# A split-precision decoder trunk on one core: another order of the seven block products in its MLP, with norm and sample work moved

## The chip, the core and the metric

The kernel runs on one core of one Trainium2 chip. The core has TensorE (matmuls into PSUM), VectorE, ScalarE, GpSimd and SyncE (SP, which here only issues DMAs), each with its own instruction queue; they meet by semaphores. The metric is the device time of one execution in microseconds (us), lower is better.

## What is computed

One step of a decoder trunk for 1024 prompt tokens and 32 sample tokens, all in float32. Mixing heads and an output projection come first; the change lies in the MLP and the last norm behind them:

```python
x = x + mix.astype(x.dtype) @ w_out
u = rmsnorm(x, g_ffn) @ w_up                  # 1024 -> 4096
x = x + jnp.square(jax.nn.relu(u)) @ w_down   # 4096 -> 1024
y_prompt = rmsnorm(hp, g_final)               # x of the prompt
y_sample = rmsnorm(hs, g_final)               # x of the sample tokens
```

## The kernel before

A float32 operand is cut in two: a high part in the format that TensorE multiplies fast (a copy with rounding, on ScalarE) and a low part, which is the operand less its high part. A product is then three matmuls, low by high, high by low, high by high. So each operand needs a high instruction on ScalarE and a low instruction on VectorE or GpSimd before TensorE can start.

The MLP (`phase_g_*`) goes through the 4096 hidden columns in 8 blocks (`NBLK`) of 4 chunks of 128 columns (`NF`). A block has two parts.

*Hidden pieces.* 12 pieces (`NU`), three token groups of 352 for each chunk (`hidden_piece`, `product`, L340 to L342). VectorE takes each from PSUM with a ReLU (L2669) into R_u, ScalarE squares it there (L2531, `squared`). Chunks of w_up arrive in R_stage, ScalarE makes their high part (L2075, `up_high`) and GpSimd the low part (L2079, `up_low`). In the last chunk of a block the groups go 2, 0, 1.

*The product with w_down.* The 32 sample tokens have a product of their own in bank 7 (`sample_product`, L350). The prompt's product is a 2 by 2 block product in seven multiplications in place of eight (Winograd's form of Strassen's scheme), the steps P1 to P7. Their left operands are quarters of R_u (q11 to q22: token half, column half) or sums of them (s2 = q22 - q21 on VectorE, L2675; three others on GpSimd), the right ones quarters of w_down in R_raw (w11 to w22) or sums of them on GpSimd (T_1 to T_4; t2 lies in R_stage). The order is P1 P2 P6 P7 P5 P3 P4. A step is four token tiles p of six matmuls (`step`, L2510 to L2512), 24 in all. Some steps open their PSUM banks, others add to what an earlier step left there; after each step VectorE adds the bank to x1 in SBUF (`added`, L2659; P7's twice, to two places). For each step ScalarE makes the high parts (left L2546, right L2554). VectorE makes the left low parts (L2649) and P6's right low part (L2686), GpSimd the other right low parts (L2600). High parts have two buffers by turns, so a step's high parts wait for the step two before it.

What sets the order is the code itself: each engine's list is written out, and `operand_high`, `right_split`, `dve_split`, `pool_sums`, `d_psum` and `d_taken` are the semaphores between them. The sample product stands behind the last piece and ahead of P1, GpSimd's weight sums wait for it (they write over R_raw), and so the sums start with P1.

*Start and end.* Four small DMAs bring the final norm's gain for the sample tokens (`g_sample`); SP issues them behind two chunks of w_up and four row blocks of w_down. VectorE waits for them ahead of the MLP's first ReLU:

```python
            dve.wait_ge(x1_in, 16 * 17)
            for b in range(NBLK):
```

At the end `final` norms the nine token tiles in the order sample, 0 to 7, within and behind P4: a sum of squares on ScalarE (L2589), mean (L2639), root on ScalarE (L2591), reciprocal (L2642), multiply (L2644), and SP stores the tile. The sample's mean needs one small matmul (L2524) that sums over token rows, between P3 and P4.

Of the kernel before, what the change touches and what calls it, by code (L numbers as in the profile page):

```python
# [151 lines left out]
def program(nc, i_, o_):  # L152

    ctx = ExitStack()
    with ctx:
# [257 lines left out]
        def phase_a_act(act):  # L413
# [33 lines left out]
            act.wait_ge(small_dve, 1)  # L447
# [54 lines left out]
        def phase_a_pe(pe):  # L502
# [15 lines left out]
            pe.wait_ge(bias_ready, 1)  # L518
# [183 lines left out]
        def phase_b_act(act):  # L702
# [110 lines left out]
        def phase_b_sync(sp):  # L813
            for s in range(NSLOTS):
# [15 lines left out]
                if s == 13:  # L830
                    sp.wait_ge(small_dve, 3)
# [1513 lines left out]
        def quarter(ap, j, i, n):  # L2345
# [18 lines left out]
        POOL_LOWS = (P1, P2, P7, P5, P3, P4)  # L2364
        S_3, T_1, T_2, T_3, T_4, S_1, S_4 = range(7)
        HIGH_ORDER = [(P1, "right"), (P2, "right"), (P1, "left"), (P2, "left"), (P6, "left"), (P6, "right")] + [
            (k, side) for k in (P7, P5, P3, P4) for side in ("right", "left")]
        DVE_ORDER = [(P1, "left"), (P2, "left"), (P6, "left"), (P6, "right"), (P7, "left"), (P5, "left"), (P3, "left"),
                     (P4, "left")]
# [4 lines left out]
        dve_split, s2_ready, pool_sums = sem("dve_split"), sem("s2_ready"), sem("pool_sums")  # L2374
# [3 lines left out]
        LAST_TILES = [NCH, 0, 1, 2, 3, 4, 5, 6, 7]  # L2378
# [46 lines left out]
        def phase_g_sync(sp):  # L2425
# [13 lines left out]
            for b in range(NBLK - 1):  # L2439
# [13 lines left out]
            for done, i in enumerate(LAST_TILES):  # L2453
# [139 lines left out]
        def phase_g_gps(pool):  # L2593
# [8 lines left out]
            for b in range(NBLK):  # L2602
# [25 lines left out]
                if not last:  # L2628
                    up_low(NF * b + 6)
# [148 lines left out]
```

## Time and profile before

| what | us |
|---|---|
| median of 3 runs (lowest, highest) | 1548.35 (1547.43, 1549.69) |
| the profiled execution, its span | 1547.07, 1545.3 |
| TensorE matmuls busy | 1455.8 (94%) |
| VectorE busy | 889.2 (58%) |
| GpSimd busy | 562.8 (36%) |
| ScalarE busy | 508.8 (33%) |

The profile is of one execution, with times counted from its first instruction. In rows and listings PE is TensorE, DVE VectorE, ACT ScalarE, POOL GpSimd and SPq SP's DMA queue. A timeline row gives start, duration, engine, line, output and inputs, and in brackets how long the engine stood idle ahead of it and what released it. Consecutive instructions of an engine overlap a little, so starts tell the pace better than durations do. Matmuls overlap more: a step matmul shows 0.39 us, but the next starts 0.23 later. The MLP runs from about 800 to 1528 us.

### The profile page before, as it was taken

Reading aid. Unit: us, or ns where it says so; the run is one execution under the profiler, and the core shown is the slowest. Engines: PE = TensorE matmul, PEld = TensorE weight load, DVE = VectorE, ACT = ScalarE, POOL = GpSimd, SP = SyncE. Lnnn points to the kernel's source line nnn. Section 1 sums busy time; section 2 is a strip of 40 time slices with the busy share of each in tenths; the row PEclk is TensorE's granted clock in tenths of the full one; section 3 lists DMA queues with packets and bytes.
Section 4 is the critical chain, followed back from the end, with each engine's and each line's share of the span. In section 5 each row is a group of like instructions: output and inputs, shape, how many; then the busy total and the mean of one; then the engine's idle time right before and its main releaser. Section 6 shows DMA issues by size and latency. Waiting matters only on the chain.

```text
span 1545.3 us, 27564 instructions
## 1 busy us (share of the span) xinstructions
PE 1455.8 (94%) x11442; PEld 1282.2 (83%) x11442; DVE 889.2 (58%) x1635; ACT 508.8 (33%) x895; POOL 562.8 (36%) x432
## 2 busy tenths in 40 slices
PE   6989999999998988999997999999999999999995
PEld 5989999999996666858887798897979889797984
DVE  6873554668844777644361735629183553818268
ACT  6343221323313677433132322222231222223124
POOL 2122222789410000014003725347383534638252
PEclk9999999999999999999998999999999999999998
DMA  7412104522118512782103110212011020201002
GB/s 215 155 53 45 29 19 92 82 78 62 54 33 332 193 56 71 285 328 90 33 1 113 55 56 28 68 28 82 28 41 55 28 69 28 82 28 42 28 14 112
DMA packets 120942, 127.22 MB, mean 82 GB/s; under 512 B 26610, under 2 KB 95030, under 8 KB 119922
## 3 DMA queue, kind: packets, MB, share of 16 engines
q1 hardware_dynamic: 118754, 120.74, 25.2%
q0 software_dynamic: 2064, 4.72, 0.8%
q8 instruction: 91, 1.49, 0.4%
q14 instruction: 33, 0.27, 0.1%
HBM read 111.17 MB, written 18.98 MB: 84 GB/s over the span
## 4 chain that ended last, share of the span: by engine, by line
PE 78%; DVE 11%; issue 7%; ACT 3%; DMA 1%; SPq 0%; POOL 0%; DVEq 0%; ACTq 0%
PE PS L340 15%; PE PS L341 14%; PE PS L342 14%; DVE R_x L2659 4%; PE PS L2510 4%; PE PS L2512 3%; PE PS L2511 3%; PE PS L1644 2%; PE PS L1665 2%; PE PS L2188 2%; PE PS L2190 2%; PE PS L2189 2%; PE PS L1684 2%; PE PS L1919 2%; PE PS L350 1%
## 5 line engine op out<-in xcount | busy, mean ns | idle before, releaser
L340 PE MATMUL PS<-x_high,R_up 128*128 128x352 f32 x768 | 249.1, 324 | 8.1 <-DVE R_u L2669 8.1
L341 PE MATMUL PS<-x_low,R_up 128*128 128x352 f32 x768 | 247.3, 322 | 0.0
L342 PE MATMUL PS<-x_high,R_up 128*128 128x352 f32 x768 | 247.1, 322 | 0.0
L2669 DVE TENSOR_SCALAR R_u<-PS 128x352 f32<-128x352 f32 x96 | 50.0, 524 | 305.0 <-PE PS L342 292.4
L2079 POOL TENSOR_TENSOR R_up<-R_stage,R_up 128x1024 fp32r<-128x1024 f32 x30 | 78.8, 2626 | 356.8 <-ACT R_up L2075 356.8
L2510 PE MATMUL PS<-R_wb,R_ua 128*128 128x512 f32 x448 | 179.9, 402 | 17.5 <-DVE R_wb L2686 12.8
L2659 DVE TENSOR_TENSOR R_x<-R_x,PS 128x512 f32<-128x512 f32 x256 | 162.7, 678 | 23.5 <-PE PS L2512 23.3
L2511 PE MATMUL PS<-R_wb,R_ua 128*128 128x512 f32 x448 | 174.8, 390 | 0.0
L2512 PE MATMUL PS<-R_wb,R_ua 128*128 128x512 f32 x448 | 174.7, 390 | 0.0
L2531 ACT ACTIVATE R_u<-R_u 128x352 f32<-128x352 f32 x96 | 47.6, 498 | 352.5 <-DVE R_u L2669 352.5
L340 PEld LDWEIGHTS PS<-x_high,R_up 128*128 128x128 f32 x768 | 145.0, 189 | 8.6 <-issue 8.4
L341 PEld LDWEIGHTS PS<-x_low,R_up 128*128 128x128 f32 x768 | 145.1, 189 | 0.3
L342 PEld LDWEIGHTS PS<-x_high,R_up 128*128 128x128 f32 x768 | 144.9, 189 | 0.0
L601 POOL TENSOR_TENSOR R_w<-R_wstage,R_w 128x1024 fp32r<-128x1024 f32 x29 | 73.6, 2538 | 177.1 <-ACT R_w L596 177.1
L2600 POOL TENSOR_TENSOR R_wb<-R_raw,R_wb 128x1024 fp32r<-128x1024 f32 x48 | 115.1, 2398 | 42.0 <-ACT R_wb L2554 42.0
L340 PE MATMUL PS<-xn_high,R_w 128*128 128x352 f32 x384 | 126.6, 330 | 3.4 <-ACT R_hscr L730 2.0
L2510 PEld LDWEIGHTS PS<-R_wb,R_ua 128*128 128x128 f32 x448 | 84.0, 187 | 51.7 <-DVE R_wb L2686 16.2
L340 PE MATMUL PS<-R_w,xn_low 128*128 128x256 f32 x432 | 124.8, 289 | 0.0
L341 PE MATMUL PS<-xn_low,R_w 128*128 128x352 f32 x384 | 123.8, 322 | 0.9 <-issue 0.9
L342 PE MATMUL PS<-xn_high,R_w 128*128 128x352 f32 x384 | 123.9, 323 | 0.0
L341 PE MATMUL PS<-R_w,xn_high 128*128 128x256 f32 x432 | 122.0, 282 | 0.0
L342 PE MATMUL PS<-R_w,xn_high 128*128 128x256 f32 x432 | 121.4, 281 | 0.0
(402 smaller groups left out, 3031.8 us busy)
## 6 DMA issues: line engine op xcount, KB each, us to landing
R_raw<-in_w_down SPq DMA_DIRECT2D x32, 512.0 KB, 4.4
R_stage<-in_w_up SPq DMA_DIRECT2D x30, 512.0 KB, 4.1
R_wstage<-in_w_in SPq DMA_DIRECT2D x28, 512.0 KB, 4.2
R_cache<-in_cache_attn_v SPq DMA_DIRECT2D x56, 256.0 KB, 9.0
R_cache<-in_cache_attn_k SPq DMA_DIRECT2D x28, 256.0 KB, 5.9
R_cache<-in_cache_attn_k SPq DMA_DIRECT2D x7, 1024.0 KB, 8.9
bias_by_distance_copies<-bias_by_distance POOLq DMA_DIRECT2D x1, 4608.0 KB, 28.0
queries_and_keys<-R_spill SPq DMA_DIRECT2D x24, 176.0 KB, 2.8
```

The costliest lines, as they stand in the source:

```text
L340: pe.matmul(out, ll, rh, start=(k == 0), stop=False)
L341: pe.matmul(out, lh, rl_, start=False, stop=False)
L342: mm = pe.matmul(out, lh, rh, start=False, stop=(k == n - 1))
L601: pool.tensor_tensor(parts_at(m)[1], wst[stage_of[m]], parts_at(m)[0].bitcast(F32), ALU.subtract)\
L2079: eng.tensor_tensor(CHUNKS[m][1], CHUNKS[m][3], CHUNKS[m][0].bitcast(F32), ALU.subtract).then_inc(chunk_split, 1)
L2510: pe.matmul(out, ul[:, f, ts], wh[:, f, :], start=(f == 0 and k in OPENS), stop=False, skip_group_check=True)
L2511: pe.matmul(out, uh[:, f, ts], wl[:, f, :], start=False, stop=False, skip_group_check=True)
L2512: mm = pe.matmul(out, uh[:, f, ts], wh[:, f, :], start=False, stop=(f == 1), skip_group_check=True)
L2531: act.activation(part, part, ACT.Square).then_inc(u_squared, 1)
L2600: pool.tensor_tensor(low, RIGHT[k], high.bitcast(F32), ALU.subtract).then_inc(right_split, 1)
L2659: ins = dve.tensor_tensor(part, part, PS[:, product_bank(k, p), :], ALU.add)
L2669: dve.tensor_scalar(U[:, F % NF, g * TG:(g + 1) * TG], PS[:, u_bank(n), 0:TG], 0.0, None, ALU.max)\
```

## The change

Seven edits in the MLP and the last norm.

1. Step order P1 P2 P6 P7 P4 P5 P3 in place of P1 P2 P6 P7 P5 P3 P4, on every engine.
2. P6's right low part goes from VectorE to GpSimd, and GpSimd makes it among the weight sums. `left_split` and `right_split` then count seven steps each.
3. The sample product stands ahead of piece 11 instead of behind it. The last chunk's groups go 2, 1, 0, so s2 and the sample's add can stand ahead of VectorE's last ReLU, and the weight sums, which wait for the sample product, follow it.
4. GpSimd's low part of the block's third chunk goes behind P3's low part, ScalarE's high parts of chunks two pieces earlier, and for the third chunk behind the steps.
5. VectorE waits for 13 instead of 17 loads ahead of the first ReLU; the wait for 17 stands in the last block, ahead of the sample tile's norm.
6. The sample tile's norm moves ahead of the last block's P1 adds, and the token sum goes to a free column of bank 7. TensorE's fourth tile of P1 waits until it is read.
7. The last tiles go in the order 4, 5, 6, 7, 0, 1, 2, 3, means and roots in pairs (4 5), (6 7), (0 1) and then alone, with VectorE's list written out so that adds and multiplies lie between a mean and its reciprocal; a second junk buffer for squares. One semaphore is replaced by counts of another (`bias_ready` by `small_dve`).

```diff
-        P1, P2, P6, P7, P5, P3, P4 = STEPS = range(7)
+        P1, P2, P6, P7, P4, P5, P3 = STEPS = range(7)
...
-        LAST_TILES = [NCH, 0, 1, 2, 3, 4, 5, 6, 7]
+        FINALS = [[NCH], [4, 5], [6, 7], [0, 1], [2], [3]]
...
-            return NF * b + f, (2, 0, 1)[u % 3] if f == NF - 1 else u % 3
+            return NF * b + f, 2 - u % 3 if f == NF - 1 else u % 3
...
-                sp.wait_ge(dve_split, dve_count(b, P6, "right"))
+                sp.wait_ge(right_split, 7 * b + P6 + 1)
                 sp.wait_ge(pool_sums, sums_count(b, T_4))
-                sp.wait_ge(chunk_split, NW + KD + NF * b + 6)
                 load_chunk(sp, KD + NF * b + 7)
-                sp.wait_ge(right_split, 6 * b + POOL_LOWS.index(P5) + 1)
+                sp.wait_ge(right_split, 7 * b + P5 + 1)
                 raw_rows(b + 1, 0)
-                sp.wait_ge(right_split, 6 * b + POOL_LOWS.index(P4) + 1)
+                sp.wait_ge(right_split, 7 * b + P3 + 1)
                 raw_rows(b + 1, 1)
...
                     if k == P1 and p == 3:
                         pe.wait_ge(d_taken, ND * b + 1)
+                        if b == NBLK - 1:
+                            pe.wait_ge(meansq_ready, 2 * NTILE + 1)
...
                     hidden_piece(pe, b, u)
-                sample_product(b)
+                    if u == NU - 2:
+                        sample_product(b)
+                if b == NBLK - 1:
+                    pe.wait_ge(sumsq_ready, 2 * NTILE + 1)
+                    pe.matmul(PS[:, 7, 256:257], token_sum, stat[:, 0, NCH:NTILE], start=True, stop=True).then_inc(token_psum, 1)
...
-            dve.wait_ge(x1_in, 16 * 17)
+            dve.wait_ge(x1_in, 16 * 13)
```

GpSimd, one middle block from the first weight sum to the last low part of its steps. R_wb are right low parts, R_raw weight sums (R_stage is t2), R_u sums of hidden quarters, R_up the third chunk. Before:

```order
L2616 TENSOR_TENSOR R_raw<-R_raw 128x2x512 [waits right_split,d_psum]
L2618 TENSOR_TENSOR R_stage<-R_raw 128x1024 [waits pool_sums]
L2619 TENSOR_TENSOR R_raw<-R_raw 128x2x512
L2621 TENSOR_TENSOR R_raw<-R_raw,R_stage 128x2x512 [waits pool_sums]
L2624 TENSOR_TENSOR R_u<-R_u,R_s2 128x2x512 [waits dve_split,s2_ready]
L2600 TENSOR_TENSOR R_wb0<-R_raw,R_wb0 128x1024 [waits operand_high]
L2626 TENSOR_TENSOR R_u<-R_u,R_s2 128x2x512
L2600 TENSOR_TENSOR R_wb1<-R_raw,R_wb1 128x1024 [waits operand_high]
L2079 TENSOR_TENSOR R_up2<-R_stage,R_up2 128x1024 [waits chunk_high]
L2600 TENSOR_TENSOR R_wb0<-R_raw,R_wb0 128x1024 [waits operand_high]
L2600 TENSOR_TENSOR R_wb1<-R_raw,R_wb1 128x1024 [waits operand_high]
```

Now:

```order
L2634 TENSOR_TENSOR R_raw<-R_raw 128x2x512 [waits right_split,d_psum]
L2636 TENSOR_TENSOR R_stage<-R_raw 128x1024 [waits pool_sums]
L2637 TENSOR_TENSOR R_raw<-R_raw 128x2x512
L2618 TENSOR_TENSOR R_wb1<-R_stage,R_wb1 128x1024 [waits operand_high]
L2640 TENSOR_TENSOR R_raw<-R_raw,R_stage 128x2x512 [waits pool_sums]
L2618 TENSOR_TENSOR R_wb0<-R_raw,R_wb0 128x1024 [waits operand_high]
L2644 TENSOR_TENSOR R_u<-R_u,R_s2 128x2x512 [waits left_split,s2_ready]
L2618 TENSOR_TENSOR R_wb1<-R_raw,R_wb1 128x1024 [waits operand_high]
L2646 TENSOR_TENSOR R_u<-R_u,R_s2 128x2x512
L2618 TENSOR_TENSOR R_wb0<-R_raw,R_wb0 128x1024 [waits operand_high]
L2618 TENSOR_TENSOR R_wb1<-R_raw,R_wb1 128x1024 [waits operand_high]
L2080 TENSOR_TENSOR R_up2<-R_stage,R_up2 128x1024 [waits chunk_high]
```

P6's low part (R_wb from R_stage) is new and stands ahead of the fourth weight sum; sums and low parts take turns from there to P5's low part, and the chunk's low part has gone behind all of them.

VectorE, one middle block from its hidden pieces to the adds of P2. L2669 and L2695 are ReLUs, R_s2 is s2, R_ua left low parts, 128x256 the sample's add, 128x512 adds of steps. Before:

```order
L2669 TENSOR_SCALAR R_u<-PS 128x352 [waits u_psum] x9
L2649 TENSOR_TENSOR R_ua0<-R_u,R_ua0 128x1024 [waits operand_high]
L2669 TENSOR_SCALAR R_u<-PS 128x352 [waits u_psum] x3
L2675 TENSOR_TENSOR R_s2<-R_u 128x1024 [waits pool_sums,u_squared]
L2649 TENSOR_TENSOR R_ua1<-R_u,R_ua1 128x1024 [waits operand_high]
L2678 TENSOR_TENSOR R_x1<-R_x1,PS 128x256 [waits d_psum]
L2659 TENSOR_TENSOR R_x1<-R_x1,PS 128x512 [waits d_taken,d_psum] x4
L2649 TENSOR_TENSOR R_ua0<-R_s2,R_ua0 128x1024 [waits operand_high,s2_ready]
L2659 TENSOR_TENSOR R_x1<-R_x1,PS 128x512 [waits d_taken,d_psum]
L2686 TENSOR_TENSOR R_wb0<-R_stage,R_wb0 128x1024 [waits operand_high]
L2659 TENSOR_TENSOR R_x1<-R_x1,PS 128x512 [waits d_taken,d_psum] x4
L2649 TENSOR_TENSOR R_ua1<-R_u,R_ua1 128x1024 [waits operand_high]
```

Now:

```order
L2695 TENSOR_SCALAR R_u<-PS 128x352 [waits u_psum] x9
L2675 TENSOR_TENSOR R_ua0<-R_u,R_ua0 128x1024 [waits operand_high]
L2695 TENSOR_SCALAR R_u<-PS 128x352 [waits u_psum] x2
L2702 TENSOR_TENSOR R_s2<-R_u 128x1024 [waits pool_sums,u_squared]
L2704 TENSOR_TENSOR R_x1<-R_x1,PS 128x256 [waits d_psum]
L2695 TENSOR_SCALAR R_u<-PS 128x352 [waits u_psum]
L2675 TENSOR_TENSOR R_ua1<-R_u,R_ua1 128x1024 [waits operand_high,u_squared]
L2685 TENSOR_TENSOR R_x1<-R_x1,PS 128x512 [waits d_taken,d_psum] x5
L2675 TENSOR_TENSOR R_ua0<-R_s2,R_ua0 128x1024 [waits operand_high,s2_ready]
L2685 TENSOR_TENSOR R_x1<-R_x1,PS 128x512 [waits d_taken,d_psum] x4
L2675 TENSOR_TENSOR R_ua1<-R_u,R_ua1 128x1024 [waits operand_high]
L2685 TENSOR_TENSOR R_x1<-R_x1,PS 128x512 [waits d_taken,d_psum] x4
```

s2 and the sample's add stand ahead of the last ReLU, P2's left low part is the only thing between that and P1's adds, and the low part into R_wb is gone.

VectorE at the end of the program, first rows of the tiles' norms (stat 128x1 or 128x2 are means and reciprocals, L2644 and L2670 multiplies, 128x512 the adds of the last step). Before:

```order
L2659 TENSOR_TENSOR R_x1<-R_x1,PS 128x512 [waits d_taken,d_psum] x4
L2639 TENSOR_SCALAR stat<-PS 128x1 [waits token_psum,sumsq_ready,x1_in]
L2642 RECIPROCAL stat<-stat 128x1 [waits rms_ready]
L2644 SCALAR_TENSOR_TENSOR R_x1<-R_x1,stat 128x256 [waits dve_order]
L2659 TENSOR_TENSOR R_x1<-R_x1,PS 128x512 [waits d_taken,d_psum]
L2639 TENSOR_SCALAR stat<-stat 128x1 [waits sumsq_ready]
L2642 RECIPROCAL stat<-stat 128x1 [waits rms_ready]
L2644 SCALAR_TENSOR_TENSOR R_x1<-R_x1,stat,R_gain 128x1024 [waits dve_order]
L2659 TENSOR_TENSOR R_x1<-R_x1,PS 128x512 [waits d_taken,d_psum]
```

Now:

```order
L2658 TENSOR_SCALAR stat<-stat 128x2 [waits sumsq_ready,x1_in]
L2685 TENSOR_TENSOR R_x1<-R_x1,PS 128x512 [waits d_taken,d_psum]
L2664 RECIPROCAL stat<-stat 128x2 [waits rms_ready]
L2670 SCALAR_TENSOR_TENSOR R_x1<-R_x1,stat,R_gain 128x1024 [waits rstd_ready]
L2658 TENSOR_SCALAR stat<-stat 128x2 [waits sumsq_ready]
L2685 TENSOR_TENSOR R_x1<-R_x1,PS 128x512 [waits d_taken,d_psum]
L2664 RECIPROCAL stat<-stat 128x2 [waits rms_ready]
L2670 SCALAR_TENSOR_TENSOR R_x1<-R_x1,stat,R_gain 128x1024 [waits rstd_ready]
L2685 TENSOR_TENSOR R_x1<-R_x1,PS 128x512 [waits d_taken,d_psum]
L2670 SCALAR_TENSOR_TENSOR R_x1<-R_x1,stat,R_gain 128x1024 [waits rstd_ready]
L2685 TENSOR_TENSOR R_x1<-R_x1,PS 128x512 [waits d_taken,d_psum]
```

A mean and its reciprocal stood next to each other; now an add of P3 lies between them, they cover two tiles, and the tiles that are normed first are 4 and 5.

## Rows read from the trace of the kernel before

**Rows 1.** The page: shares of the chain that ended last; first step matmul's group.

```profile
PE 78%; DVE 11%; issue 7%; ACT 3%; DMA 1%; SPq 0%; POOL 0%; DVEq 0%; ACTq 0%
L2510 PE MATMUL PS<-R_wb,R_ua 128*128 128x512 f32 x448 | 179.9, 402 | 17.5 <-DVE R_wb L2686 12.8
```

**Rows 2.** Timeline in front of the MLP: VectorE, TensorE, SP.

```profile
824.11 1.81 DVE L2669 TENSOR_SCALAR R_u<-PS 128x352 f32<-128x352 f32 x4 [12.59 <-DMA R_x<-in_g_final]
...
816.35 0.32 PE L342 MATMUL PS<-x_high,R_up 128*128 128x352 f32 x1
824.78 0.63 PE L340 MATMUL PS<-x_high,R_up 128*128 128x352 f32 x1 [8.11 <-DVE R_u L2669]
...
830.35 0.33 PE L341 MATMUL PS<-x_low,R_up 128*128 128x352 f32 x1
...
811.60 1.01 SPq L2071 DMA_DIRECT2D R_stage<-in_w_up  x2
```

**Rows 3.** Busy time by stretch; the first line names the columns.

```profile
core 0: us, PE busy (x) PEld busy (x) DVE busy (x) ACT busy (x) POOL busy (x), PEclk, DMA share, GB/s
...
825.00:832.00 7.00, 7.00 (x30) 7.00 (x31) 1.45 (x4) 3.37 (x7) 2.38 (x1) 0.63 0.21 60
```

**Rows 4.** The same view, one steady block from P1 to the next P1.

```profile
949.45:1039.01 89.56, 87.28 (x490) 77.88 (x489) 47.14 (x55) 23.74 (x31) 45.48 (x17) 1.00 0.15 48
```

**Rows 5.** Timeline of the same block: VectorE, ScalarE, GpSimd.

```profile
936.62 1.31 DVE L2649 TENSOR_TENSOR R_ua<-R_u,R_ua 128x1024 fp32r<-128x1024 f32 x1
...
947.62 0.53 DVE L2669 TENSOR_SCALAR R_u<-PS 128x352 f32<-128x352 f32 x1 [3.29 <-PE PS L342]
...
949.86 3.42 DVE L2649 TENSOR_TENSOR R_ua<-R_u,R_ua 128x1024 fp32r<-128x1024 f32 x1
...
953.53 2.51 DVE L2659 TENSOR_TENSOR R_x<-R_x,PS 128x512 f32<-128x512 f32 x4
...
955.36 1.06 ACT L2546 ACTIVATE R_ua<-R_s 128x1024 fp32r<-128x1024 f32 x1 [5.58 <-PE PS L2512]
...
949.56 2.63 POOL L2616 TENSOR_TENSOR R_raw<-R_raw 128x1024 f32<-128x1024 f32 x1 [1.29 <-PE PS L350]
...
964.54 2.40 POOL L2600 TENSOR_TENSOR R_wb<-R_raw,R_wb 128x1024 fp32r<-128x1024 f32 x1
966.89 3.40 POOL L2626 TENSOR_TENSOR R_u<-R_u,R_s 128x1024 f32<-128x1024 f32 x1
970.25 2.40 POOL L2600 TENSOR_TENSOR R_wb<-R_raw,R_wb 128x1024 fp32r<-128x1024 f32 x1
```

**Rows 6.** Timeline of the same block: TensorE.

```profile
947.52 1.93 PE L350 MATMUL PS<-R_raw,R_u 128*32 128x256 f32 x32
949.38 0.50 PE L2510 MATMUL PS<-R_wb,R_ua 128*128 128x512 f32 x1
...
955.16 0.39 PE L2510 MATMUL PS<-R_wb,R_ua 128*128 128x512 f32 x1
...
960.37 0.39 PE L2512 MATMUL PS<-R_wb,R_ua 128*128 128x512 f32 x1
962.37 0.50 PE L2510 MATMUL PS<-R_wb,R_ua 128*128 128x512 f32 x1 [1.61 <-DVE R_wb L2686]
...
979.14 0.39 PE L2512 MATMUL PS<-R_wb,R_ua 128*128 128x512 f32 x1
980.19 0.47 PE L2510 MATMUL PS<-R_wb,R_ua 128*128 128x512 f32 x1 [0.66 <-DVE R_x L2659]
```

**Rows 7.** Timeline at the end: TensorE's last matmul, VectorE's last two multiplies.

```profile
1527.70 0.39 PE L2512 MATMUL PS<-R_wb,R_ua 128*128 128x512 f32 x1
...
1538.97 1.28 DVE L2644 SCALAR_TENSOR_TENSOR R_x<-R_x,stat,R_gain 128x1024 f32<-128x1024 f32 x1
1540.79 1.28 DVE L2644 SCALAR_TENSOR_TENSOR R_x<-R_x,stat,R_gain 128x1024 f32<-128x1024 f32 x1
```

**Rows 8.** DMA issues from 811.5 to 812.0: line's tile, count, size, us to landing.

```profile
R_stage<-in_w_up SPq DMA_DIRECT2D x1, 512.0 KB, 4.6
```

More of the change, by code:

```diff
@@ L2363, in program @@
         ND = 1 + 7 * 4
-        POOL_LOWS = (P1, P2, P7, P5, P3, P4)
         S_3, T_1, T_2, T_3, T_4, S_1, S_4 = range(7)
[L2366 to L2369, printed above, removed]
+        HIGH_ORDER = [(P1, "right"), (P2, "right"), (P1, "left"), (P2, "left")] + [
+            (k, side) for k in (P6, P7, P4, P5, P3) for side in ("right", "left")]
         u_psum, u_relu, u_squared = sem("u_psum"), sem("u_relu"), sem("u_squared")
@@ L2494, in step @@
             def step(b, k):
-                pe.wait_ge(dve_split, dve_count(b, k, "right" if k == P6 else "left"))
-                if k != P6:
-                    pe.wait_ge(right_split, 6 * b + POOL_LOWS.index(k) + 1)
+                pe.wait_ge(left_split, 7 * b + k + 1)
+                pe.wait_ge(right_split, 7 * b + k + 1)
                 (uh, ul), (wh, wl) = ua[(7 * b + k) % 2], wb[(7 * b + k) % 2]
@@ L2559, in phase_g_act @@
                 for u in range(NU):
+                    if u == 11 and last:
+                        tile_squares(NCH)
                     squared(b * NU + u)
@@ L2571, in phase_g_act @@
                         left_high_part(b, P1)
[L2572 to L2573 removed]
+                    if u in (5, 8) and not last:
+                        up_high(NF * b + 4 + (u - 5) // 3)
                 act.wait_ge(u_squared, NU * b + NU)
                 left_high_part(b, P2)
[L2576 to L2578 removed]
+                if last:
+                    roots(0)
+                for k in (P6, P7, P4, P5, P3):
                     right_high_part(b, k)
                     left_high_part(b, k)
[L2581 to L2591 removed]
+                if not last:
+                    up_high(NF * b + 6)
+            tile_squares(4)
+            tile_squares(5)
+            roots(1)
+            tile_squares(6)
+            tile_squares(7)
+            roots(2)
+            tile_squares(0)
+            tile_squares(1)
+            roots(3)
+            tile_squares(2)
+            roots(4)
+            tile_squares(3)
+            roots(5)
         def phase_g_gps(pool):
@@ L2693, in phase_g_dve @@
                 added(b, P7, 0)
-                left_low_part(b, P5)
+                left_low_part(b, P4)
                 for p in range(1, 4):
                     added(b, P7, p)
-                left_low_part(b, P3)
-                for p in range(4):
-                    added(b, P5, p)
-                added(b, P3, 0)
-                left_low_part(b, P4)
-                for p in range(1, 4):
-                    added(b, P3, p)
+                left_low_part(b, P5)
                 for p in range(4):
                     added(b, P4, p)
-                    if last:
-                        if p == 0:
-                            dve.wait_ge(x1_in, 16 * 18)
-                        final(LAST_TILES[p])
-            for i in LAST_TILES[4:]:
-                final(i)
+                added(b, P5, 0)
+                left_low_part(b, P3)
+                for p in range(1, 4):
+                    added(b, P5, p)
+                if not last:
+                    for p in range(4):
+                        added(b, P3, p)
+            b = NBLK - 1
+            dve.wait_ge(x1_in, 16 * 18)
+            statistics(1)
+            added(b, P3, 0)
+            reciprocals(1)
+            scaled(4)
+            statistics(2)
+            added(b, P3, 1)
+            reciprocals(2)
+            scaled(5)
+            added(b, P3, 2)
+            scaled(6)
+            added(b, P3, 3)
+            statistics(3)
+            scaled(7)
+            reciprocals(3)
+            scaled(0)
+            statistics(4)
+            scaled(1)
+            reciprocals(4)
+            scaled(2)
+            statistics(5)
+            reciprocals(5)
+            scaled(3)
         PHASES = {
```

115 lines of the change are left out of this document (60 added, 55 removed).

## The prediction

> **What bounds the kernel now.** First the chain of work that ended last on the page: 78% of the span is TensorE [rows 1]. So a change pays only where TensorE stands still, or behind its last matmul. The page has two such places by name, the idle time of the step matmuls before L2510 [rows 1] and, in the timeline, one hole in front of the MLP [rows 2]. Then I read the stretches.
>
> The opening of the MLP: VectorE idles 12.59 us and is released by the DMA of g_final; TensorE stands from 816.35 to 824.78 and is released by VectorE's first ReLU [rows 2]. The granted clock from 825 to 832 is 0.63 [rows 3]; the matmuls behind the hole run at the lower level, 1.2 GHz, and are at their old pace from 830.35 on.
>
> One steady block takes 89.56 us [rows 4]. A ReLU comes 3.29 us idle and 0.53 of work after the last, 3.81 with their overlap [rows 5], so 12 hidden pieces are 45.7. The sample product is 1.86 from its start to the first step matmul [rows 6], with its start gap 1.95. A step is 24 matmuls; 23 of them lie between 955.16 and 960.37 [rows 6], 0.227 each, so a step is 5.45 and seven are 38.15. The sum is 85.8, so TensorE loses about 3.75 us in a block. Two holes can be named: 1.77 before P6 (wait 1.61 for VectorE's right low part) and 0.82 before P3 (wait 0.66 for an add) [rows 6]; the other 1.2 are restarts of 0.1 to 0.2 at P1's fourth tile, P6, P7 and P5.
>
> Behind the last matmul (starts 1527.70) VectorE takes 1.82 us for a tile [rows 7], and the last multiply ends at 1542.07, 14.0 us after the last matmul's end at 1528.09; 3.2 us of store follow.
>
> **The change part by part.** Times are those of the profiled execution, 1547.07 us, 1.3 below the median of 1548.35.
>
> *Norm weight wait moved down.* VectorE's first ReLU then waits only for loads that it had already waited for, and can start at 811.5, when its last part of x is done. TensorE, which finished four pieces at 816.5, goes straight on. Gone are 8.27 (816.35 to 824.78 less a pace of 0.16) and the slow matmuls: 19 from 824.78 to 830.35 in 5.57 instead of 3.02, so 2.55. Sum 10.8. What is late next: the weight chunk of piece 6. Its load is issued at 811.60 and lands 4.6 later [rows 2, 8], with 1.04 on ScalarE and 2.4 on GpSimd it is split by 819.8; piece 6 is due at 816.5 + 2 x 3.81 = 824.1. The w_down rows land before the g_final pieces queued behind them, so by 824.1, and ScalarE, which stands for them, holds up no ReLU; the sample product is due at 843. Bounds: 8.3 if the clock falls for another reason, 10.9 at most.
>
> *P6's right low part goes from VectorE to GpSimd, the sample product and s2 move ahead of piece 11.* These are one question: are VectorE and GpSimd still ready for each step? I walk one block, counted from the sample product's start. Piece 11 ends and P1 starts at 1.86 + 3.81 + 0.08 = 5.75; the steps are due at 11.2 (P2), 16.65 (P6), 22.1 (P7), 27.55 (P4), 33.0 (P5), 38.45 (P3). The rows show how the two engines share: a left low part alone takes 1.31, but 3.42 when a GpSimd instruction is under way, and it ends 1.08 after that one; the GpSimd instruction queued behind takes 3.40 instead of 2.40 [rows 5]. So they alternate, 2.4 low, 1.08 left low, 2.3 sum, and two low parts with a sum between start 5.71 apart (964.54, 970.25) [rows 5].
> The first weight sum starts 2.04 after the sample product in both kernels [rows 5, 6], which is now 3.81 earlier against P1: three sums are done at 9.45, P2's left low part at 10.5 (due 11.2). ScalarE makes P6's high part when P1 is out: 955.36 less 949.38 is 5.98, of which 0.16 is the fourth tile's wait that goes [rows 5, 6]; so at 11.55, done 12.6. GpSimd: P6 low 12.7 to 15.1, left low 16.2 (due 16.65). Then 5.71 for each step: left lows at 21.9 for P7 (due 22.1), 27.6 for P4 (27.55), 33.3 for P5 (33.0). P3 has no sum ahead of it: low 37.85 at the latest, left low 38.95 against 38.5 plus what P5 was late, so just in time. Adds: four take 2.51 [rows 5], P7's are double; P7's last is taken at 31.3, P4's fourth tile wants it at 31.6. The margins are tenths; none is a microsecond.
> So there remain per block 0.17 (restarts around the sample product), 0.1 at P4, 0.45 at P5 with its restart, 0.15 elsewhere: 0.87 instead of 3.75, a gain of 2.9. From below: if each of P7, P4 and P5 is 0.3 later than walked, 2.0. From above: every restart gone but the first, 3.5. Nearest is the walk, since its 5.71 is a measured spacing. Blocks 0 to 6: 7 x 2.9 = 20.3.
>
> *Step order.* P4 now comes right behind P7 and waits for its double adds; P3 is last, and the next block's first four pieces take its banks. P3's first tile is taken 2 us before that piece starts, the others each a piece's time ahead: no cost. GpSimd's up_low of the third chunk, now behind P3's low part, ends near 41 and is wanted at piece 6 of the next block, 26 us later. SP's loads behind it (w_down rows after P5 and P3, three chunks) move by at most 2 us and land some 20 us before use. Chunk high parts two pieces earlier on ScalarE, renamed semaphores and the dropped SP wait: nothing, they stand in ScalarE's and SP's idle time.
>
> *Last block.* Sample norm moved up: TensorE's fourth tile of P1 waits until VectorE has read the token sum, which stands behind P2's left low part at 10.5; wanted at 10.0, given at 10.75 with restart, so 0.8 lost. Before, this block lacked the P3 hole (0.8). Gain 2.9 - 0.8 - 0.8 = 1.3 (0 to 2).
> ScalarE's square root now stands between copies, ahead of P6's high part. In the rows behind the steps a root and a square alternate within VectorE's 1.82 a tile [rows 7], so I count 0.2. The Trainium skill (ScalarE: Activation LUTs, section "Table sets: the hidden batching unit") says that functions of different sets cost a table load of about 2.7 us at each switch; an estimate by that page of two loads would put the last block up to 5 us later, 1517 in place of 1512. The rows speak against it: no room for a load in 1.82.
>
> *Tail.* Tiles 4 to 7 are whole after P5 and can be normed while P3 runs; means and roots go in pairs, and VectorE does other work in the round trip to ScalarE. After the last matmul VectorE has six multiplies at 1.22 (7.3), two adds (1.25), five small ones (0.6) and one round trip (0.6): 9.75 instead of 14.0, a gain of 4.2. Stores follow at 1.3 to 1.8 us, the last with 1.8 of room as before. If ScalarE's squares come late, 3; if the stores run closer, 5.
>
> Sum: 10.8 + 20.3 + 1.3 + 4.2 = 36.6; 1547.07 - 36.6 = 1510.5, against the median some 1512.
>
> **The rivals.**
> *A GpSimd instruction slips in once per block.* If one left low part (say P4's, asked for at 25.2 while P4's low part runs to 26.5) is asked for too late, the next sum goes first: 2.3 late, and the chain of 5.71 can't win it back against 5.45. For: the margins above. Against: in the block read, every left low part came directly behind the GpSimd instruction that it met. Price 8 x 2.2 = 18: 1530. Chance 0.10.
> *The opening stops again.* Something else of the opening (a late chunk, ScalarE held by w_down) stops TensorE for 4 to 5 us and the clock falls again: 1512 + 7 = 1519. Against: 4 us of margin at piece 6. Chance 0.12.
> *Slower: GpSimd keeps the port.* With one more low part, GpSimd's queue has no gap from T_4 to P5. If VectorE's left low parts of P7, P4 and P5 each wait for two instructions, 1.08 + 2 x 2.38 = 5.8, VectorE has 20.1 of adds (32 at 0.63) + 3 x 5.8 + 3 x 2.4 = 44.7 us in 38.15 of steps and becomes the bound: some 5.8 us a block more than walked, 46 in all: 1558. It turns the sign from 4.6 us a block on, a mean left low part of some 3.9 us. Chance 0.02. The Trainium skill (SBUF — State Buffer, section "Who interferes with whom") has the rule behind it: whoever issues first keeps the shared port pair for its whole instruction, and it names no turn-taking; by it 1558 is possible. The trace shows turns: 3.42 is one instruction's rest and 1.08, not two.
> *The change doesn't do what it says*: the hole at 816 is not the wait's. Then 1512 + 10.8 = 1523; VectorE's releaser row speaks against it. Chance 0.03.
>
> **How the numbers follow.** Forecast (1512, own range 1506 to 1518) 0.73, the rivals 0.10, 0.12, 0.02, 0.03. Low end: 3.5 a block and 5 in the tail, 1512 - 4.2 - 0.8 - 0.7 = 1506. High end: the stopped opening with 2.5 a block, 1519 + 3 = 1522; outside lie the two port rivals, 1523, and a little of the forecast. A measurement here tells 0.2%, 3 us, from no change. Faster 0.97, same 0.01, slower 0.02.
>
> **What will show it.** VectorE's first ReLU at about 811.6 with no DMA as releaser, TensorE's granted clock 1.00 from 811 to 832; block spacing near 86.7; waits before P6 and P3 gone, a few tenths for a left low part before P4 or P5; left low parts no longer than 3.5; last multiply some 10 us after the last matmul. A spacing above 88 or a TensorE hole between 816 and 845 would make it wrong.

## The result and the profile after

The changed kernel takes 1508.11 us (median of 4 runs, 1507.10 to 1508.62), the kernel before, in the same comparison, 1547.89 (1546.24 to 1549.69). The ratio is 0.974, its 95% interval 0.9725 to 0.9759. The profiled execution takes 1508.5 us with a span of 1506.7; before it was 1547.07 with 1545.3.

The stretch ahead of the MLP's first ReLU holds the same instructions in both kernels, so I count from a common mark there: the first of the last full group of transposes, which stands among the MLP's first matmuls. These two rows, one of before and one of after, are TensorE's timeline there (start and duration in us, engine, line, operation, output and inputs):

```profile
803.86 0.31 PE L2250 MATMUL PS<-ident,R_xs 128*128 128x128 f32 x1
```

```profile
804.18 0.31 PE L2251 MATMUL PS<-ident,R_xs 128*128 128x128 f32 x1
```

From the mark to the span's end it is 741.4 us before and 702.5 after, 38.9 less. This splits as follows (us; a sample product is counted by its first matmul's start):

| stretch | before | after | gain | forecast |
|---|---|---|---|---|
| mark to first sample product (after: with 3.81 for the piece that now follows it) | 54.09 | 43.34 | 10.75 | 10.8 |
| seven times the spacing of the blocks | 7 x 89.57 | 7 x 86.41 | 22.1 | 20.3 |
| last sample product to last matmul's end (after: less that piece, 3.81) | 43.16 | 41.68 | 1.48 | 1.3 |
| last matmul's end to last multiply's end | 13.98 | 9.48 | 4.50 | 4.2 |

The stores behind the last multiply give the remaining 0.06 (3.23 before, 3.17 after).

The page answers [rows 1] so: first the shares of the chain that ended last, then the group of the first step matmul (instructions, busy time, mean ns, idle time before and its releaser).

```profile
PE 62%; DVE 3%; issue 1%; DMA 1%; ACT 0%; SPq 0%; DVEq 0%
...
L2507 PE MATMUL PS<-R_wb,R_ua 128*128 128x512 f32 x448 | 176.4, 394 | 0.5 <-DVE stat L2658 0.5
```

The idle time of this group went from 17.5 us to 0.5, and VectorE's right low part is no longer a releaser. The shares of this chain add up to 67% only: it is followed back no further than 485 us, so they can't be set beside those of [rows 1]. A second profile of the same kernel (the run under "Two ways to more") has the chain back to 3 us:

```profile
PE 90%; DVE 4%; ACT 2%; issue 2%; DMA 1%; SPq 0%; POOL 0%; DVEq 0%; ACTq 0%
```

There VectorE's share is 4% in place of 11%, and TensorE's 90% in place of 78%.

The timeline of the opening, VectorE and then TensorE, answers [rows 2]:

```profile
811.76 0.95 DVE L2695 TENSOR_SCALAR R_u<-PS 128x352 f32<-128x352 f32 x2
813.19 0.52 DVE L2695 TENSOR_SCALAR R_u<-PS 128x352 f32<-128x352 f32 x1 [0.48 <-PE PS L343]
...
816.35 0.32 PE L341 MATMUL PS<-x_high,R_up 128*128 128x352 f32 x1
816.51 0.32 PE L342 MATMUL PS<-x_low,R_up 128*128 128x352 f32 x1
```

The first ReLU starts at 811.76 and waits for no DMA. TensorE passes 816.35, where it stood for 8.27 us, at its usual 0.16. The view by stretch answers [rows 3 and 4], with its line of columns:

```profile
core 0: us, PE busy (x) PEld busy (x) DVE busy (x) ACT busy (x) POOL busy (x), PEclk, DMA share, GB/s
825.00:832.00 7.00, 7.00 (x45) 7.00 (x45) 0.77 (x2) 4.10 (x6) 5.20 (x3) 1.00 0.19 49
849.65:936.05 86.40, 86.40 (x490) 78.11 (x489) 42.80 (x53) 23.74 (x30) 47.06 (x19) 1.00 0.17 49
```

From 825 to 832 the granted clock is 1.00 instead of 0.63, and 45 matmuls run where 30 did. A block is 86.40 us with the same 490 matmuls, and TensorE's busy time is the whole of it; losses of a few tenths between steps (below) don't show in this figure, since the spans of matmuls overlap.

### The profile page after: what moved, and what is told of

It is laid out like the page before. It is cut to its first block, busy times and chain, and to the rows that moved or that the text cites. A ratio compares the mean times of both kernels' runs of the same rounds, so it can differ in the third digit from the quotient of the medians.

```text
span 1506.7 us, 27571 instructions
## 1 busy us (share of the span) xinstructions
PE 1447.3 (96%) x11442; PEld 1283.9 (85%) x11442; DVE 853.1 (57%) x1621; ACT 509.1 (34%) x892; POOL 577.9 (38%) x440
## 4 chain that ended last, share of the span: by engine, by line
PE 62%; DVE 3%; issue 1%; DMA 1%; ACT 0%; SPq 0%; DVEq 0%
PE PS L341 8%; PE PS L342 8%; PE PS L343 8%; PE PS L2507 7%; PE PS L2508 7%; PE PS L2509 7%; PE PS L1666 2%; PE PS L1645 2%; PE PS L2189 2%; PE PS L2191 2%; PE PS L2190 2%; PE PS L1685 2%; PE PS L1920 2%; PE PS L351 1%; PE PS L1930 1%
## 5 line engine op out<-in xcount | busy, mean ns | idle before, releaser
L2695 DVE TENSOR_SCALAR R_u<-PS 128x352 f32<-128x352 f32 x96 | 50.3, 525 | 294.2 <-PE PS L343 294.2
L2685 DVE TENSOR_TENSOR R_x<-R_x,PS 128x512 f32<-128x512 f32 x256 | 161.1, 677 | 22.9 <-PE PS L2509 22.1
L2675 DVE TENSOR_TENSOR R_ua<-R_u,R_ua 128x1024 fp32r<-128x1024 f32 x48 | 106.2, 2213 | 14.2 <-ACT R_ua L2543 14.2
```

What stands on the lines that cost most here:

```text
L2675: dve.tensor_tensor(low, LEFT[k], high.bitcast(F32), ALU.subtract).then_inc(left_split, 1)
L2685: ins = dve.tensor_tensor(part, part, PS[:, product_bank(k, p), :], ALU.add)
L2695: dve.tensor_scalar(U[:, F % NF, g * TG:(g + 1) * TG], PS[:, u_bank(n), 0:TG], 0.0, None, ALU.max)\
```

## The experiments

Each kernel is the changed one with the edit shown, but for the first, which is the kernel before with one edit. For each stands the median of its runs and what its profile gives by the marks of the table. The theory is the prediction's: four gains that don't depend on each other, and margins of tenths for VectorE and GpSimd in each block.

**The wait alone, in the kernel before.**

```diff
-            dve.wait_ge(x1_in, 16 * 17)
+            dve.wait_ge(x1_in, 16 * 13)
```

> The kernel before with one number changed: VectorE waits for 13 loads, not 17, ahead of the MLP's first ReLU. Theory (the hole at 816 us is that wait and nothing else, 8.3 us of standing and 2.3 of slow clock): 10.6 us less than before, about 1537.3, TensorE without a hole from 811 to 832 at a granted clock of 1.00, block spacing still 89.6. Rival (the next load is nearly as late): a second hole of 4 to 5 us opens and the clock falls again, about 1544.

1534.46 us (1533.69 to 1536.06), ratio 0.992 (0.9902 to 0.9935). From the mark it gains 10.8 us, all of it ahead of the first sample product (845.95 − 802.60 = 43.35 in place of 54.09); the blocks stay at 89.56. The stretch of [rows 3] in this kernel:

```profile
825.00:832.00 7.00, 7.00 (x46) 7.00 (x45) 1.05 (x2) 2.61 (x5) 6.41 (x3) 1.00 0.28 77
```

So the one number in the wait removes both the hole and the lower clock behind it.

**The wait put back.**

```diff
-            dve.wait_ge(x1_in, 16 * 13)
+            dve.wait_ge(x1_in, 16 * 17)
```

> The changed kernel with the old wait for 17 loads put back. Theory: the opening's share does not depend on the rest, so 10.6 us more than the changed kernel, about 1518.7, with VectorE released by the DMA of g_final and block spacing still 86.4. Rival (the other edits of the first block already hide part of the wait, as ScalarE's and GpSimd's lists start otherwise): 5 us more or less than that.

1519.0 us (1517.79 to 1519.88); 10.2 us longer from the mark, with blocks of 86.39. VectorE's timeline has the releaser of [rows 2] again:

```profile
823.98 1.82 DVE L2695 TENSOR_SCALAR R_u<-PS 128x352 f32<-128x352 f32 x4 [12.70 <-DMA R_x<-in_g_final]
```

The gain is 10.8 without the rest of the change and 10.2 with it: the parts add up to within 0.6.

**The sample product late again**, in blocks 0 to 6.

```diff
-                    if u == NU - 2:
+                    if u == (NU - 2 if b == NBLK - 1 else NU - 1):
                         sample_product(b)
...
+                    if u == (10 if last else 11):
                         dve.wait_ge(d_psum, ND * b + 1)
                         dve.tensor_tensor(x1s, x1s, PS[:, 7, 0:256], ALU.add).then_inc(d_taken, 1)
```

> The changed kernel with the sample product behind the last piece again in blocks 0 to 6 (the last block as changed). Theory (the 3.8 us of lead for the weight sums is what the P6 low part on GpSimd lives on): by the walk the three sums end 8.3 us after P1's start, P6's left low part at 11.8 against 10.9 due, P6 1.0 late, P7, P4 and P5 0.3 each: 1.7 us a block more than changed, spacing 88.1, in all 12 us, about 1520. Rival (GpSimd has slack enough, the gain came from VectorE's relief): spacing 86.4 to 86.8, 1508 to 1511.

1518.83 us (1518.19 to 1521.42), 9.1 longer from the mark; blocks of 87.71, 1.30 more each, where I had worked out 1.7. TensorE at P6:

```profile
949.71 0.47 PE L2507 MATMUL PS<-R_wb,R_ua 128*128 128x512 f32 x1 [0.56 <-issue]
```

There is one hole of 0.72 before P6, where 1.0 was worked out, and then about 0.3 more at each of P7, P4 and P5: GpSimd's chain has lost its lead, and as its low parts come 5.71 apart and the steps every 5.45, each step behind P6 waits for the difference.

**P6's right low part on VectorE again**, the early sample product kept.

```diff
-                right_low_part(b, P6)
...
                 left_low_part(b, P6)
+                dve.wait_ge(operand_high, high_count(b, P6, "right"))
+                high, low = wb[(7 * b + P6) % 2]
+                dve.tensor_tensor(low, t2, high.bitcast(F32), ALU.subtract).then_inc(p6_right, 1)
```

> The changed kernel with P6's right low part back on VectorE, behind P6's left low part; GpSimd's list without it, else as changed. Theory (with the sample product early GpSimd has nothing in hand when VectorE makes the two low parts, so they take 1.2 each and end at 16.2 against 16.6 due): spacing 86.4, about 1508, plus or minus 1. Rival (VectorE's list was the cause of the 1.77 us hole, whatever the sums do): the hole comes back, 1.8 us a block, spacing 88.2, about 1522.

1505.7 us (1504.76 to 1512.34). By time this is the changed kernel's; from the mark it is 1.3 us shorter, with blocks of 86.12 in place of 86.41. So this part of the change costs a little where the sample product is early. VectorE's and GpSimd's rows at P6 in this kernel:

```profile
941.44 1.23 DVE L2682 TENSOR_TENSOR R_ua<-R_s,R_ua 128x1024 fp32r<-128x1024 f32 x1
942.58 1.22 DVE L2726 TENSOR_TENSOR R_wb<-R_stage,R_wb 128x1024 fp32r<-128x1024 f32 x1
...
945.90 2.40 POOL L2626 TENSOR_TENSOR R_wb<-R_raw,R_wb 128x1024 fp32r<-128x1024 f32 x1 [5.17 <-ACT R_wb L2559]
```

and GpSimd's at the same place in the changed kernel:

```profile
942.70 2.41 POOL L2618 TENSOR_TENSOR R_wb<-R_stage,R_wb 128x1024 fp32r<-128x1024 f32 x1 [3.09 <-ACT R_wb L2551]
945.07 3.39 POOL L2640 TENSOR_TENSOR R_raw<-R_raw,R_stage 128x1024 f32<-128x1024 f32 x1
948.41 2.42 POOL L2618 TENSOR_TENSOR R_wb<-R_raw,R_wb 128x1024 fp32r<-128x1024 f32 x1
```

With P6's low part gone from GpSimd, its sums are done early, it stands idle for 5.17 us, and VectorE's two low parts at P6 meet nobody (1.23 and 1.22). P7's low part starts 18.03 us after the sample product in place of 18.30, and the 0.27 that P5 waited (see the section on why the prediction was right) is gone.

The last block is 0.4 longer here. VectorE's multiply of the sample tile, then GpSimd's row beside it, and the same multiply in the changed kernel:

```profile
1455.73 1.99 DVE L2677 SCALAR_TENSOR_TENSOR R_x<-R_x,stat 128x256 f32<-128x256 f32 x1
...
1454.08 3.36 POOL L2647 TENSOR_TENSOR R_raw<-R_raw,R_stage 128x1024 f32<-128x1024 f32 x1
```

```profile
1459.71 0.48 DVE L2670 SCALAR_TENSOR_TENSOR R_x<-R_x,stat 128x256 f32<-128x256 f32 x1
```

The multiply takes 1.99 instead of 0.48, since it meets a weight sum on GpSimd, and P6 then waits 0.76.

**Both of these back**: the two edits above in one kernel.

> The changed kernel with both edits undone in blocks 0 to 6: sample product behind the last piece and P6's right low part on VectorE. Theory (the hole of 1.8 us before P6 came from the weight sums running while P6's parts were wanted, and VectorE's low part had to wait for a whole GpSimd sum): the hole is back, spacing 88.0 to 88.3, 12 to 14 us more than changed. Rival (P6 on GpSimd is what matters and the earlier run on VectorE was faster only by the shorter GpSimd list): 87.7 as with the late sample alone, or less.

1521.52 us (1519.78 to 1521.73), 12.8 longer from the mark; blocks of 88.15. VectorE, GpSimd and TensorE at P6:

```profile
947.05 3.40 DVE L2727 TENSOR_TENSOR R_wb<-R_stage,R_wb 128x1024 fp32r<-128x1024 f32 x1
...
945.98 3.40 POOL L2647 TENSOR_TENSOR R_raw<-R_raw,R_stage 128x1024 f32<-128x1024 f32 x1
...
950.56 0.47 PE L2515 MATMUL PS<-R_wb,R_ua 128*128 128x512 f32 x1 [1.64 <-issue]
```

This is the hole of [rows 6] again, with its cause: the low part on VectorE starts while GpSimd makes a sum, and lasts 3.40 instead of 1.22. The four kernels make a table of block spacings:

| us per block | low part on VectorE | low part on GpSimd |
|---|---|---|
| sample product late | 88.15 | 87.71 |
| sample product early | 86.12 | 86.41 |

The early sample product is worth 2.03 or 1.30. The low part's move to GpSimd saves 0.44 beside a late one and costs 0.29 beside an early one: either edit takes away the same meeting of VectorE and GpSimd at P6, and the second to be made has little or nothing left to save there.

The kernel before has 89.57, so 1.42 a block is still between it and this one. The step order, taken back alone in the next experiment, is worth 0.66 of it. The other 0.76 belongs to edits that no run took back (the order of the last groups, s2 ahead of the last ReLU, the chunk parts that moved), or the order is worth more beside a late sample product; no run tells which.

**The old step order**, last tiles in the order 0 to 7 with it.

```diff
-        P1, P2, P6, P7, P4, P5, P3 = STEPS = range(7)
+        P1, P2, P6, P7, P5, P3, P4 = STEPS = range(7)
```

> The changed kernel with the old step order P5 P3 P4 behind P7 in all blocks (lists of all engines, and the last tiles in the order 0 to 7 since P4 is last then). Theory (P5's adds stand behind P7's double ones and P3 wants the first of them): the hole of 0.8 to 1.1 before P3 comes back, P5 less late by 0.3: spacing 86.9 to 87.4, 4 to 8 us more, 1512 to 1516. Rival (the hole before P3 came from P6's delay and is gone with it): spacing 86.4, 1508.

1513.96 us (1512.82 to 1517.09), 5.2 longer from the mark; blocks of 87.07, 0.66 more. TensorE at P3:

```profile
964.95 0.47 PE L2507 MATMUL PS<-R_wb,R_ua 128*128 128x512 f32 x1 [0.67 <-DVE R_x L2685]
```

The second hole of [rows 6] is back with its old size (a wait of 0.67, before 0.66) and its old releaser, an add. A block is longer by about that hole, so closing it is what the new order is worth beside the other edits.

**Margins: 1.03 us more on GpSimd**, in the chain of the steps, and behind it. A subtraction of an unused 128x512 tile stands ahead of P7's low part in one kernel, behind P3's low part in the other.

```diff
+                pool.tensor_tensor(R_dum, R_dum, R_dum, ALU.subtract).then_inc(dum_done, 1)
                 right_low_part(b, P7)
```

> The changed kernel with one GpSimd instruction more in each block, a 128x512 subtraction of some 1.2 us into unused memory, ahead of P7's low part. It adds work that the result doesn't need. Theory (the margins from P7 to P5 are tenths): P7 about 1.0 late, the delay stays to P5, 1.2 us a block more, spacing 87.6, about 1518. Rival (GpSimd and VectorE have a microsecond in hand there): spacing under 86.7, 1508 to 1510.

```diff
                 right_low_part(b, P3)
+                pool.tensor_tensor(R_dum, R_dum, R_dum, ALU.subtract).then_inc(dum_done, 1)
```

> The same extra GpSimd instruction, but behind P3's low part, where no step waits for it. Theory: nothing, spacing 86.4, 1508 plus or minus 1. Rival (any GpSimd work costs, by the port or by VectorE's adds): part of the cost of the other place.

The first: 1515.33 us (1513.54 to 1515.73), 7.7 longer from the mark, 0.97 a block. The second: 1507.45 (1505.43 to 1509.78), 0.0 longer from the mark, 0.0 a block. GpSimd's added row and TensorE's answer in the first kernel:

```profile
948.93 1.03 POOL L2645 TENSOR_TENSOR R_dum<-R_dum 128x512 f32<-128x512 f32 x1
...
953.40 0.47 PE L2508 MATMUL PS<-R_wb,R_ua 128*128 128x512 f32 x1 [0.49 <-issue]
```

So GpSimd's chain from P7's low part to P5's has no slack: of 1.03 us put into it, 0.97 lengthen the block. Ahead of P6's low part it has 3.09 us of idle time (the row above), and behind P3's there is room for at least 1 us. A late operand cost what was added, not a whole further instruction of 2.4. It was GpSimd that was made late here, though: a left low part that VectorE asks for too late, as in the first port rival, was not tried.

**The tail one tile at a time**, in the new order.

```diff
-        FINALS = [[NCH], [4, 5], [6, 7], [0, 1], [2], [3]]
+        FINALS = [[NCH], [4], [5], [6], [7], [0], [1], [2], [3]]
...
+            for n in range(5, 9):
+                statistics(n)
+                reciprocals(n)
+                scaled(FINALS[n][0])
```

> The changed kernel with the last eight tiles normed one by one in the order 4 to 7, 0 to 3: mean, root, reciprocal, multiply each behind the other on VectorE, as before the change. Theory: a tile costs 1.8 us again instead of 1.2 to 1.4, so the stretch from the last matmul's end to the last multiply is 12 to 14 us instead of 9.5: 2.5 to 4.5 us more, 1511 to 1513. Rival (the gain of the end is that four tiles are whole before the last step, not the pairs): under 1.5 us more.

1509.16 us (1508.85 to 1515.74). Its median is only 1.05 above that of the changed kernel, but from the mark it is 3.5 longer, all of it behind the last matmul: 13.02 us in place of 9.48. The last two multiplies, first of this kernel and then of the changed one:

```profile
1500.80 1.29 DVE L2660 SCALAR_TENSOR_TENSOR R_x<-R_x,stat,R_gain 128x1024 f32<-128x1024 f32 x1
...
1502.62 1.28 DVE L2660 SCALAR_TENSOR_TENSOR R_x<-R_x,stat,R_gain 128x1024 f32<-128x1024 f32 x1
```

```profile
1500.47 1.28 DVE L2670 SCALAR_TENSOR_TENSOR R_x<-R_x,stat,R_gain 128x1024 f32<-128x1024 f32 x1
...
1502.08 0.17 DVE L2664 RECIPROCAL stat<-stat 128x1 f32<-128x1 f32 x1 [0.27 <-ACT stat L2566]
1502.28 1.28 DVE L2670 SCALAR_TENSOR_TENSOR R_x<-R_x,stat,R_gain 128x1024 f32<-128x1024 f32 x1
```

A multiply every 1.82 again, as in [rows 7], for every tile; in the changed kernel only the last tile pays the round trip to ScalarE, whose visible part is 0.27. The new tile order, one tile at a time, gives 0.96 of the 4.50 (13.98 to 13.02), the interleaving 3.54.

**Two ways to more.** The changed kernel once more beside them:

> The changed kernel itself, for a comparison on one chip with the next two. 1506 to 1510, block spacing 86.4; the stretch ahead of the MLP may be a microsecond or two longer or shorter than in the first profile, since the same code took 796.1 to 800.2 us to its end in the runs so far.

1506.34 us (1505.69 to 1512.77), 702.4 from the mark. The first way makes the sum T_4 ahead of P6's low part on GpSimd, and in the last block takes the sample tile's mean ahead of P2's left low part:

```diff
-                right_low_part(b, P6)
                 pool.wait_ge(pool_sums, sums_count(b, T_2))
                 pool.tensor_tensor(w21, w21, t2, ALU.subtract).then_inc(pool_sums, 1)
+                right_low_part(b, P6)
...
-                dve.wait_ge(u_squared, NU * (b + 1))
-                left_low_part(b, P2)
                 if last:
                     dve.wait_ge(x1_in, 16 * 17)
                     statistics(0)
+                dve.wait_ge(u_squared, NU * (b + 1))
+                left_low_part(b, P2)
```

> The changed kernel with the fourth weight sum ahead of P6's low part on GpSimd, and in the last block the sample's mean ahead of P2's left low part on VectorE. Theory (GpSimd stands idle for 3.1 us ahead of P6's low part, and one sum fits in; the chain to P5 is then one sum shorter): P6 on time with 0.2 in hand, P4 and P5 no longer late, 0.3 us a block less, spacing 86.1, and 0.65 less at P1's fourth tile of the last block: 2.5 to 3 us less than changed. Rival (P6's low part, now behind the sum, becomes late instead): spacing 86.4 to 86.7.

1505.21 us (1502.98 to 1511.70), 700.1 from the mark, blocks of 86.12. The view by stretch for one of its blocks, and GpSimd's two rows at P6:

```profile
855.25:941.37 86.12, 86.12 (x490) 78.19 (x489) 42.60 (x53) 23.73 (x30) 47.04 (x19) 1.00 0.16 50
```

```profile
944.88 3.41 POOL L2639 TENSOR_TENSOR R_raw<-R_raw,R_stage 128x1024 f32<-128x1024 f32 x1
948.23 2.40 POOL L2618 TENSOR_TENSOR R_wb<-R_stage,R_wb 128x1024 fp32r<-128x1024 f32 x1
```

The second way is the kernel with P6's low part on VectorE, with the sample tile's norm taken apart so that its multiply meets no sum:

```diff
-                dve.wait_ge(u_squared, NU * (b + 1))
-                left_low_part(b, P2)
                 if last:
                     dve.wait_ge(x1_in, 16 * 17)
                     statistics(0)
-                    reciprocals(0)
-                    scaled(NCH)
+                dve.wait_ge(u_squared, NU * (b + 1))
+                left_low_part(b, P2)
...
+                if last:
+                    reciprocals(0)
+                    scaled(NCH)
```

> P6's right low part on VectorE as in the earlier run, and the last block mended: the sample's mean ahead of P2's left low part, its reciprocal and multiply behind P6's two low parts, where GpSimd stands idle. Theory: spacing 86.12, in the last block the wait of 0.66 at P1's fourth tile and the one of 0.76 ahead of P6 gone: 3 us less than changed, 1505 or a little under. Rival (the last block's lists are bound by VectorE's adds anyway): 1.5 less.

1505.28 us (1502.65 to 1509.96), 699.6 from the mark, blocks of 86.13, last sample product to last matmul's end 44.39 in place of 45.49. From the mark both are shorter than the changed kernel beside them (by 2.3 and 2.8 us) and than the one with P6's low part on VectorE (701.2). By medians it is 1.1 against the changed kernel, and the runs overlap, so the times alone don't tell them apart from it.

## Why the prediction was right

It said 1512 within 1506 to 1522; it came out at 1508, by the mechanism named for each part. Step by step:

**What bounds the kernel.** TensorE's holes were the right place to look: 34.3 of the 38.9 us are holes closed and the clock that one of them had cost, the rest is the tail. The parts were forecast at 36.6 together.

**Opening, 10.8: 10.75.** The wait alone gave 10.8 in the kernel before, and put back took 10.2. The next load was met as walked: the chunk of piece 6 lands 4.9 after its issue (the forecast used 4.6, [rows 8]); ScalarE and GpSimd take it thus:

```profile
816.94 1.06 ACT L2076 ACTIVATE R_up<-R_stage 128x1024 fp32r<-128x1024 f32 x1 [3.68 <-DMA R_stage<-in_w_up]
818.08 2.39 POOL L2080 TENSOR_TENSOR R_up<-R_stage,R_up 128x1024 fp32r<-128x1024 f32 x1 [88.43 <-ACT R_up L2076]
```

It is split at 820.5, due at 824.1. So neither the rival of a second stop nor that of another cause came about. That the clock fell because of the hole was argued from [rows 2, 3]; the first experiment shows it, since with the hole gone the granted clock is 1.00.

**Blocks, 2.9 each: 3.16.** The walk held to about 0.1 us. Counted from the sample product, which starts at 930.11 (first row below), GpSimd's low part of P6 starts at 12.6 (forecast 12.7); the left low parts end at 16.1 (16.2), 21.8 (21.9), 27.5 (27.6) and 33.2 (33.3). Behind that row stand VectorE's four, P6, P7, P4 and P5, and then TensorE at P4, P5 and P3, each behind the last matmul of the step before:

```profile
930.11 1.93 PE L351 MATMUL PS<-R_raw,R_u 128*32 128x256 f32 x32
...
943.67 2.52 DVE L2675 TENSOR_TENSOR R_ua<-R_s,R_ua 128x1024 fp32r<-128x1024 f32 x1
...
949.04 2.86 DVE L2675 TENSOR_TENSOR R_ua<-R_u,R_ua 128x1024 fp32r<-128x1024 f32 x1
...
955.00 2.62 DVE L2675 TENSOR_TENSOR R_ua<-R_u,R_ua 128x1024 fp32r<-128x1024 f32 x1
...
961.13 2.22 DVE L2675 TENSOR_TENSOR R_ua<-R_u,R_ua 128x1024 fp32r<-128x1024 f32 x1
```

```profile
957.45 0.39 PE L2509 MATMUL PS<-R_wb,R_ua 128*128 128x512 f32 x1
957.68 0.49 PE L2507 MATMUL PS<-R_wb,R_ua 128*128 128x512 f32 x1
...
963.01 0.39 PE L2509 MATMUL PS<-R_wb,R_ua 128*128 128x512 f32 x1
963.40 0.50 PE L2507 MATMUL PS<-R_wb,R_ua 128*128 128x512 f32 x1
...
968.79 0.39 PE L2509 MATMUL PS<-R_wb,R_ua 128*128 128x512 f32 x1
969.01 0.39 PE L2507 MATMUL PS<-R_wb,R_ua 128*128 128x512 f32 x1
```

The longest of these left low parts is 2.86, so neither port rival came about: the slower one needed 5.8 for each, the other a weight sum slipped in ahead of one. One figure of the slower rival was wrong: a mean left low part of 3.9 would only just fill the block (20.1 + 3 x 3.9 + 7.2 = 39.0, against 38.15 of steps and the 0.87 forecast as lost); to turn the sign it would take some 5.4. The mis-sized term is what remains: 0.87 forecast, 0.6 measured (86.41 less the 85.8 of pieces, sample product and steps). P4 and P5 were priced at 0.55 together and cost 0.43. P5 starts 0.27 later than P4's start and a step would have it (5.72 less 5.45), and its own restart takes 0.16 (5.61 from its start to P3's, less 5.45): that is the 0.45 forecast for P5. But P4's restart of 0.10 lies within the 0.27, as P5 waits for its left low part at 33.2 and not for P4; the forecast counted it a second time. And the 0.15 "elsewhere" is not there.

**One step was right only as a sum.** The prediction took the low part's move and the earlier sample product as one question and gave them one price. The table of four shows that the sample product carries it: alone it gives 2.03 a block, and with the move 1.74 (88.15 to 86.41). The walk's margins of tenths were spent by the move itself: GpSimd's chain is what was late at P5, and without that low part in it, or with a sum moved out of its way, the block comes to 86.12.

**Last block, 1.3: 1.48.** TensorE's fourth tile of P1 waits as forecast; VectorE's mean, TensorE's row and ScalarE's root:

```profile
1459.10 0.14 DVE L2658 TENSOR_SCALAR stat<-PS 128x1 f32<-128x1 f32 x1
...
1459.39 0.47 PE L2507 MATMUL PS<-R_wb,R_ua 128*128 128x512 f32 x1 [0.52 <-DVE stat L2658]
...
1459.28 0.20 ACT L2566 ACTIVATE stat<-stat 128x1 f32<-128x1 f32 x1 [2.55 <-DVE stat L2658]
1461.05 1.06 ACT L2551 ACTIVATE R_wb<-R_stage 128x1024 fp32r<-128x1024 f32 x1 [1.57 <-PE PS L2509]
```

The loss is 0.68, forecast 0.8. The root takes 0.20 and starts 0.04 behind the mean; the copy behind it waits 1.57 for TensorE. A table load is a row of its own in these traces. There are 14 in the profile, each 1.28 us long; the last stands ahead of the first root of the norm in front of the MLP:

```profile
728.43 1.28 ACT L2283 ACT_TABLE_LOAD   x1
729.72 0.20 ACT L2283 ACTIVATE stat<-stat 128x1 f32<-128x1 f32 x1
```

Behind it, copies, squares and roots follow each other without another load, in the MLP and in the last norm. The Trainium skill (ScalarE: Activation LUTs, section "Table sets: the hidden batching unit") gives about 2.7 us for a table load at a switch of sets; the load of these rows takes 1.28 and the root starts at its end, and the estimate of 1517 by that page did not come about, as there is no load here to pay for.

**Tail, 4.2: 4.50.** The interleaving was priced by VectorE's work alone, 9.75 for 9.48. The stores took 3.17 behind the last multiply, 3.23 before.

**Against the range.** The low end, 1506, is where nearly every restart is gone, 3.5 a block. Both last kernels come close to that block (86.12 and 86.13, 3.4 under the kernel before), and their medians are 1505.2 and 1505.3.

## What to carry to other kernels

When two engines meet at a port, write down for each step when its operand is due and when the chain delivers it, with the spacing that the trace shows for the pair; here it came out to 0.1 us. Walk each placing of a small piece of work that you can choose from: I walked the low part on GpSimd alone, and so did not see that it is 0.29 a block cheaper on VectorE once the sample product is early. Two edits that remove the same meeting don't add up: make the one that starts the whole chain earlier, then ask whether the other still pays. A wait with too high a count at the head of a loop can cost more than the time that the engine stands, here 10.8 us for a hole of 8.3: look at the granted clock behind the hole.

## What the runs showed of the hardware beyond that

**The port goes by turns for other instructions too.** The sample tile's multiply, 128x256 with two tensor inputs, took 0.48 alone and 1.99 beside a GpSimd sum, ending 0.28 after it; the low part on VectorE took 1.22 alone and 3.40 beside one. The Trainium skill (SBUF — State Buffer, section "Who interferes with whom") says that a VectorE instruction with two SBUF inputs contends with a GpSimd one that reads SBUF; the rows agree. In every meeting read here VectorE got the port directly behind the one instruction that it met, and GpSimd's next one waited in turn (3.39 and 3.41 in place of 2.40).

**The time ahead of the MLP varies by more than some of the effects.** The mark lay between 801.02 and 809.77 us in the profiles, with the same instructions ahead of it, while three profiles gave 702.5, 702.4 and 702.5 from it (the changed kernel twice, and the one with GpSimd's extra work behind P3, for which no step waits). So medians differ by some us where the traces agree to 0.1, as for the serial tail. What varies there was not pursued and stays open.
